# A decoder trunk on one core: the value and gate slabs of the mLSTM by seven products, in pieces between attention steps

## The reference

```python
h = rmsnorm(x, attn_norm_g)
(q, k_c, v_c, k_s, v_s, k_w, v_w, g_nsa, mq, mk, mv, mo, mi, mf, cu) = jnp.split(h @ w_in, points, axis=-1)
a_out = head_rmsnorm(nsa_attention(q, k_c, ..., g_nsa, ...), 16, nsa_out_g)      # width 1024
hm = mlstm_chunkwise(mq, mk, mv, mi + i_bias, mf + f_bias)                       # width 512
hm = head_rmsnorm(jax.nn.sigmoid(mo) * hm, 4, mlstm_out_g)
c = silu(layernorm(conv(ca * sigmoid(cg))))                                      # width 512
x = x + jnp.concatenate([a_out, hm, c], axis=-1) @ w_out
x = x + hier_moe(rmsnorm(x, ffn_norm_g), ...)                                    # 32 experts, 2 per token
return rmsnorm(x, final_norm_g)
```

## Time and profile before

| | us |
|---|---|
| median of 3 runs | 1427.34 |
| lowest, highest | 1425.18, 1428.28 |
| the profiled execution | 1428.03 |
| its span, first to last instruction | 1426.2 |

### The profile page before, as it was taken

One profiled execution on the slowest core, in us unless ns is written; L12 is line 12 of the kernel. 1 busy time (PEld: TensorE's weight loads), 2 busy tenths in 40 slices (PEclk: granted clock), 3 DMA queues, 4 the chain that ended last, 5 costly groups with the idle time before them and its releaser, 6 DMA issues.

```text
span 1426.2 us, 17903 instructions
## 1 busy us (share of the span) xinstructions
PE 1205.7 (85%) x7431; PEld 708.9 (50%) x7431; DVE 483.6 (34%) x1001; ACT 255.3 (18%) x629; POOL 13.5 (1%) x82
## 2 busy tenths in 40 slices
PE   8999999999999998669689958768587695876977
PEld 7999999766568753123244314224142241422422
DVE  5398997663875431121110220111101111011123
ACT  2101111444600122011111101002020010201112
POOL 2000000000010000000000000000000000000000
PEclk9999999999999999889999989989899898998989
DMA  9958677431644899999999999999999999999995
GB/s 318 274 158 194 167 161 236 119 82 38 165 112 166 346 413 426 429 427 427 428 428 428 426 428 427 427 427 429 428 426 427 429 427 425 431 426 426 429 427 237
DMA packets 133362, 479.34 MB, mean 336 GB/s; under 512 B 47804, under 2 KB 105632, under 8 KB 107552
## 3 DMA queue, kind: packets, MB, share of 16 engines
q1 hardware_dynamic: 126816, 477.58, 85.9%
q10 hardware_dynamic: 6464, 0.58, 0.4%
HBM read 476.05 MB, written 2.10 MB: 335 GB/s over the span
## 4 chain that ended last, share of the span: by engine, by line
PE 52%; DMA 43%; ACTq 2%; DVE 1%; ACT 1%; issue 1%; DVEq 0%
DMA ring<-in_expert_w_up_dram 36%; PE PS L1127 13%; PE PS L1447 10%; DMA spare<-in_expert_w_up_dram 6%; PE PS L1269 5%; PE PS L1169 3%; PE PS L1434 3%; PE PS L1246 2%; PE PS L1638 2%; ACTq L1862 2%; PE PS L1425 1%; PE PS L1221 1%; PE PS L1119 1%; PE PS L1648 1%; PE PS L1188 1%; PE PS L1509 1%
## 5 line engine op out<-in xcount | busy, mean ns | idle before, releaser
L1447 PE MATMUL PS<-ring,XG 128*32 128x512 f32 x1296 | 222.2, 734 | 147.9 <-DMA ring<-in_expert_w_up_dram 107.3
L1447 PEld LDWEIGHTS PS<-ring,XG 128*32 128x32 f32 x1296 | 57.6, 131 | 274.9 <-issue 271.8
L3068 DVE TENSOR_TENSOR hTe<-PS,sg 128x128 f32<-128x128 f32 (+1 forms) x31 | 9.9, 320 | 349.3 <-ACT sg L2193 349.1
L2885 DVE TENSOR_TENSOR x<-PS,x 128x1024 f32<-128x1024 f32 x41 | 50.2, 1225 | 209.8 <-PE PS L1526 208.4
L2181 ACT ACTIVATE Hs<-PS 128x512 f32<-128x512 f32 x30 | 17.9, 597 | 463.1 <-PE PS L1447 349.8
L1434 PE MATMUL PS<-ring,XG 128*64 128x512 f32 x192 | 84.6, 594 | 18.0 <-DMA ring<-in_expert_w_up_dram 14.5
L1526 PE MATMUL PS<-Y,SW 128*128 128x512 f32 (+2 forms) x176 | 90.6, 627 | 1.5 <-ACT ro L2289 1.5
L1447 PE MATMUL PS<-spare,XG 128*32 128x512 f32 x208 | 66.0, 793 | 27.8 <-DMA ring<-in_expert_w_up_dram 27.8
L1436 PE MATMUL PS<-ring,XG 128*64 128x512 f32 x192 | 85.0, 595 | 0.0
L1425 PEld LDWEIGHTS PS<-sel,xn 128*128 128x128 f32 x640 | 75.3, 191 | 13.0 <-issue 12.7
L1425 PE MATMUL PS<-sel,xn 128*128 128x128 f32 x640 | 77.6, 280 | 1.4 <-DVE x L2885 1.4
(11 more groups left out here) (494 smaller groups left out, 1577.2 us busy)
## 6 DMA issues: line engine op xcount, KB each, us to landing
ring<-in_expert_w_up_dram SPq DMA_DIRECT2D x53, 2048.0 KB, 23.8
ring<-in_expert_w_gate_dram SPq DMA_DIRECT2D x53, 2048.0 KB, 26.9
ring<-in_expert_w_down_dram SPq DMA_DIRECT2D x51, 2048.0 KB, 27.1
ring<-in_w_in_dram SPq DMA_DIRECT2D x17, 2048.0 KB, 9.5
spare<-in_expert_w_gate_dram SPq DMA_DIRECT2D x9, 2048.0 KB, 26.2
spare<-in_expert_w_up_dram SPq DMA_DIRECT2D x8, 2048.0 KB, 23.9
spare<-in_expert_w_down_dram SPq DMA_DIRECT2D x8, 2048.0 KB, 27.3
ring<-in_w_in_dram SPq DMA_DIRECT2D x16, 512.0 KB, 7.3
```

Of the source, the lines that this page charges most:

```text
L1447: mm = pe.matmul(PS[r:r + 32, 0, :], gathered_rows(q, 4 * c + j)[:, column:column + 32], weight_rows(slots[u], 4 * (c % 2) + j), start=(c ...
L2885: dve.tensor_tensor(y, new, old, ALU.add).then_inc(sc_added, 1)
```

## The change

The four late slabs join `FAST_SLABS`: they are made by the seven products too. A filler step is now a matmul of 128 columns, and there are 4 x 7 x 8 = 224 of them (before: 128 of 256 columns). The numbers of fillers given to each place are new. The four weight differences of slab 0 (`mv0`) are made by VectorE ahead of `biases(0)`, those of slabs 1 to 3 by GpSimd. The results are combined by VectorE in two parts, `late_first` (four operations) and `late_last` (four), placed between the pieces of the attention; ScalarE's eight copies go. `mlstm_values`, the output projection and the gate's sigmoid now wait for these combinations. Since the token sums stay needed in `x1`, the scores of odd steps lie in ring slot 1, and the differences in ring slot 2; so the pairs of slots of the output weights and of the expert chunks are renumbered. The second read of `x` is issued earlier, right behind the second pair of output weights. The third pair waits until the attention has turned its last block (before, it waited for units only, and the fourth had this wait); the fourth waits for `out_done`, as before. In the diff, "..." stands for lines left out: ScalarE's `late_saves` and its calls, and the branches of `save_unit` for `mv` and `mo`, are removed in them.

```diff
@@ -188,7 +188,8 @@
-FAST_SLABS = ("ca0", "ca1", "mq0", "mq1", "mk0", "mk1", "vc0", "ks0", "kw0", "vs0", "q0", "q1", "q2", "q3", "vw0")
+FAST_SLABS = ("ca0", "ca1", "mq0", "mq1", "mk0", "mk1", "vc0", "ks0", "kw0", "vs0", "q0", "q1", "q2", "q3", "vw0",
+              "mv0", "mv1", "mo0", "mo1")
 SUMS_BEFORE, PRODUCTS_BEFORE, TOKEN_SUMS = 4 * len(FAST), 2 * len(FAST), 4
...
 LATE = units_before("mv")
+LATE_SLABS = [u for u in FAST if u >= LATE]
+FAST_LATE = len(FAST) - len(LATE_SLABS)
+LATE_PRODUCTS = ["m2", "m1", "m6", "m7", "m5", "m3", "m4"]
+LATE_STEPS = 8 * len(LATE_PRODUCTS) * len(LATE_SLABS)
+SCALED = 2 + FAST_LATE
+LATE_SAVED = SCALED + 2 * len(LATE_SLABS)
...
-OUT_SLOTS = [(1, 2), (3, 4), (0, 5), (1, 2)]
+OUT_SLOTS = [(3, 4), (5, 0), (1, 2), (3, 4)]
...
-CHUNK_SLOT = [3, 4, 0, 5, 1, 2]
+CHUNK_SLOT = [5, 0, 1, 2, 3, 4]
...
-TURN = [SPARE, 3, 4, 0, 5, 1, 2]
+TURN = [SPARE, 5, 0, 1, 2, 3, 4]
...
         sc = [tile.rearrange("p (g h b k) -> p g h b k", g=2, h=HPG, b=2)
-              for tile in (att[:, :], x1[:, :, :].rearrange("p t d -> p (t d)"))]
+              for tile in (att[:, :], ring[:, 1, :, :].rearrange("p k n -> p (k n)"))]
...
+        late_sums = ring[:, 2, :, :].rearrange("p k n -> p (k n)").rearrange("p (s a k n) -> p s a k n", s=2, a=2, k=8)
+        late_a, late_b = upto[:, :], cmask[:, :]
+
+        def late_part(name):
+
+            q = LATE_PRODUCTS.index(name)
+            return PS[:, q // 4, P * (q % 4):P * (q % 4) + P]
...
             last_use = {n % RING: units_through(n) for n in range(len(SLABS))}
             for m, pair in enumerate(OUT_SLOTS):
-                if m < 3:
+                if m < 2:
                     sp.wait_ge(unit_done, max(last_use[s] for s in pair))
-                else:
-                    sp.wait_ge(p_turned, 2 * PAIRS_BY[-1])
+                elif m == 2:
                     for t in range(TT):
                         sp.dma_start(x1[:, t, :], x[0, t * P:(t + 1) * P, :]).then_inc(x_again, 16)
+                    sp.wait_ge(p_turned, 2 * PAIRS_BY[-1])
+                else:
                     sp.wait_ge(out_done, TT)
...
+            def late_sums_of(i):
+
+                j, u = FAST_LATE + i, LATE_SLABS[i]
+                n = UNITS[u][0]
+                pool.wait_ge(w_loaded[n % RING], slab_at[n])
+                pool.wait_ge(w_summed, 4 * j)
+                if i > 1:
+                    pool.wait_ge(unit_done, LATE_SLABS[i - 2] + 2)
+                pool.tensor_tensor(late_sums[:, i % 2, 0], quarter(u, 1, 1), quarter(u, 0, 1), ALU.subtract)\
+                    .then_inc(w_summed, 1)
+                pool.wait_ge(w_summed, 4 * j + 1)
+                pool.tensor_tensor(quarter(u, 0, 1), quarter(u, 0, 1), quarter(u, 0, 0), ALU.subtract)\
+                    .then_inc(w_summed, 1)
+                pool.wait_ge(w_summed, 4 * j + 2)
+                pool.tensor_tensor(late_sums[:, i % 2, 1], quarter(u, 1, 1), quarter(u, 0, 1), ALU.subtract)\
+                    .then_inc(w_summed, 1)
+                pool.wait_ge(prod_done, 2 * j + 1)
+                pool.wait_ge(w_summed, 4 * j + 3)
+                pool.tensor_tensor(quarter(u, 1, 0), quarter(u, 1, 0), late_sums[:, i % 2, 1], ALU.subtract)\
+                    .then_inc(w_summed, 1)
+
+            for i in range(1, len(LATE_SLABS)):
+                late_sums_of(i)
+
             pool.wait_ge(out_done, TT)
             step(pool.memset(lg_t, 0.0))
...
             def mlstm_values():
-                pe.wait_ge(unit_saved, units_with("mv"))
+                pe.wait_ge(first_scaled, SCALED + 4)
                 pe.wait_ge(biased, TILES_BY[-1])
...
             def late_step():
 
-                u, k = LATE + late[0] // DK, late[0] % DK
-                n, part, kind, s, i = UNITS[u]
+                i, r = divmod(late[0], 8 * len(LATE_PRODUCTS))
+                name, k = LATE_PRODUCTS[r // 8], r % 8
+                j, u = FAST_LATE + i, LATE_SLABS[i]
+                n = UNITS[u][0]
                 if k == 0:
-                    pe.wait_ge(w_loaded[n % RING], slab_at[n])
-                    pe.wait_ge(unit_saved, LATE - 2 if u == LATE else u - 1)
-                mm = pe.matmul(PS[:, unit_bank(u), 0:256], hT[:, k, i * P:(i + 1) * P], ring[:, n % RING, k, :],
-                               start=(k == 0), stop=(k == DK - 1))
-                if k == DK - 1:
+                    if name == "m2":
+                        pe.wait_ge(w_loaded[n % RING], slab_at[n])
+                    if name == "m2":
+                        pe.wait_ge(first_scaled if i else unit_saved, SCALED + 2 * i - 1 if i else LATE - 2)
+                    if name == "m5":
+                        pe.wait_ge(first_scaled if i else unit_saved, SCALED + 2 * i if i else LATE)
+                    if name in ("m6", "m4"):
+                        pe.wait_ge(w_summed, 4 * j + {"m6": 3, "m4": 4}[name])
+                tokens, weights = {"m1": (tok_11, quarter(u, 0, 0)), "m2": (tok_12, quarter(u, 1, 0)),
+                                   "m3": (tok_s4, quarter(u, 1, 1)), "m4": (tok_22, quarter(u, 1, 0)),
+                                   "m5": (tok_s1, quarter(u, 0, 1)), "m6": (tok_s2, late_sums[:, i % 2, 1]),
+                                   "m7": (tok_s3, late_sums[:, i % 2, 0])}[name]
+                mm = pe.matmul(late_part(name), tokens[:, k], weights[:, k], start=(k == 0), stop=(k == 7))
+                if k == 7 and name in ("m2", "m7"):
+                    mm.then_inc(prod_done, 1)
+                if k == 7 and name in ("m3", "m4"):
                     mm.then_inc(unit_done, 1)
                 late[0] += 1
...
-            fill(8)
+            fill(16)
             pe.wait_ge(unit_saved, LATE)
             pe.wait_ge(cmp_saved, 1)
-            scores(0, 2)
-            scores(1, 3)
-            fill(16)
+            scores(0, 6)
+            scores(1, 6)
+            fill(28)
             pe.wait_ge(sT_ready, ML_H)
-            attend(0, 4)
+            attend(0, 5)
             scores(2, 3)
-            attend(1, 4)
+            attend(1, 5)
             mean_square(0)
-            scores(3, 3)
+            scores(3, 5)
             fill(LATE_STEPS)
             mlstm_values()
             pe.wait_ge(conv_out, CT)
-            pe.wait_ge(unit_saved, len(UNITS))
+            pe.wait_ge(first_scaled, LATE_SAVED)
             out_part(0, conv_f, True, False)
...
-            exponents(0, 0)
-            late_saves(1)
-            exponents(1, 1)
-            late_saves(2)
-            attend_saves(0, 1)
-            exponents(2, 0)
-            late_saves(1)
-            attend_saves(1, 1)
+            exponents(0)
+            exponents(1)
+            attend_saves(0)
+            exponents(2)
+            attend_saves(1)
             head_root(0)
-            exponents(3, 0)
-            late_saves(1)
-            act.wait_ge(unit_saved, len(UNITS))
+            exponents(3)
+            act.wait_ge(first_scaled, LATE_SAVED)
             act.activation(mo[:, :, :], mo[:, :, :], ACT.Sigmoid, bias=ZERO_C).then_inc(mo_gated, 1)
             head_root(1)
-            attend_saves(2, 0)
-            attend_saves(3, 0)
+            attend_saves(2)
...
-            def biases(s):
+            def biases(s, slab=None):
...
                     dve.wait_ge(biased, 2 * pairs[0])
                     dve.tensor_reduce(rs[:, u, 0, :, i, 1:3], sc[u][:, :, i, :, 0:w], AX, ALU.max, negate=True)\
                         .then_inc(max_ready, 1)
+                    if i == 2 and slab is not None:
+                        late_first(slab)
...
-            biases(0)
-            biases(1)
+            def first_late_sums():
+
+                j, u = FAST_LATE, LATE_SLABS[0]
+                n = UNITS[u][0]
+                dve.wait_ge(w_loaded[n % RING], slab_at[n])
+                dve.wait_ge(unit_done, LATE)
+                dve.tensor_tensor(late_sums[:, 0, 0], quarter(u, 1, 1), quarter(u, 0, 1), ALU.subtract).then_inc(w_summed, 1)
+                dve.wait_ge(w_summed, 4 * j + 1)
+                dve.tensor_tensor(quarter(u, 0, 1), quarter(u, 0, 1), quarter(u, 0, 0), ALU.subtract).then_inc(w_summed, 1)
+                dve.wait_ge(w_summed, 4 * j + 2)
+                dve.tensor_tensor(late_sums[:, 0, 1], quarter(u, 1, 1), quarter(u, 0, 1), ALU.subtract).then_inc(w_summed, 1)
+                dve.wait_ge(prod_done, 2 * j + 1)
+                dve.wait_ge(w_summed, 4 * j + 3)
+                dve.tensor_tensor(quarter(u, 1, 0), quarter(u, 1, 0), late_sums[:, 0, 1], ALU.subtract).then_inc(w_summed, 1)
+
+            def late_first(i):
+
+                _, part, _, s, _ = UNITS[LATE_SLABS[i]]
+                dst, c = mv if part == "mv" else mo, 256 * s
+                dve.wait_ge(prod_done, 2 * (FAST_LATE + i) + 2)
+                step(dve.tensor_copy(late_a, late_part("m1")))
+                issued(dve.tensor_tensor(dst[:, 0, c:c + P], late_part("m2"), late_a, ALU.add))
```

(63 more changed lines are left out.)

## The result

| | before | after |
|---|---|---|
| median, us | 1426.55 (6 runs) | 1438.32 (6 runs) |
| lowest, highest | 1424.21, 1428.28 | 1436.93, 1440.05 |
| ratio of the times | | 1.008 (95%: 1.0069 to 1.0091) |
| the profiled execution | 1428.03 | 1440.05 |
| its span | 1426.2 | 1437.9 |

The change makes the kernel slower by 11.8 us. The forecast was slower by 4.1, with a range that ended at 1437.

What follows compares the result with a forecast made beforehand. TensorE at full clock was taken to bound the stretch. Passes and waits gave -1.6 us, GpSimd's holds +5.7, together +4.1: the median of 1427.34 becomes 1431.4, with a range of 1423 to 1437.

Steps and rivals of the forecast that it cites:

- Parts 1 and 2: TensorE's shorter filler passes (5.0 us back) and the attention stretch replayed against VectorE: sum -1.6 us.
- Part 3: SyncE's loads and the renumbered slots: output weights and `x` land before they are wanted, so nothing.
- part 4: GpSimd's twelve differences, 2.3 us each, hold up VectorE's scalings and two-tensor SBUF operations: 5.7 us taken, from 3.4 to 12.8.
- (a): Slab 1's last difference holds VectorE's L2630, ahead of late_last(0) and biases(1): 1.3 us taken, 3.8 with a second entry.
- (b): Slab 2's last difference and slab 3's three hold VectorE in gated(0), which attend(0) waits for: 4.3 us, two entries.
- (c): Slab 3's last difference, at scores(2)'s end, holds L2630 and reaches ScalarE's copies: 0.1 us.
- Rival B: VectorE isn't held up by GpSimd: 1425.7 us, with errors 1423.5 to 1427.5; chance 0.27.
- C: Faster outright, VectorE's new pieces find room everywhere: -6.6 us, half of it at least, 1421 to 1424; chance 0.10.
- D: GpSimd's operations take 3.3 us, every hold a microsecond longer: +7, up to +13, 1434 to 1440; chance 0.08.
- each time GpSimd can: In gated(0), GpSimd gets in at every chance: a hold of 8.9 us, where 4.3 was taken.
- worst case of both places: Upper end of the summed GpSimd holds on VectorE in the attention stretch: 12.8 us, where 5.7 was taken.

Runs made afterwards that it cites:

- the separated version: Changed kernel with one more wait ahead of GpSimd's last difference of each slab, behind VectorE's operations: 1424.97 us, ratio 0.9983 to before; second set 1425.33, 0.9992.
- only (b) separated: Changed kernel with one added wait: slab 2's last GpSimd difference waits until gated(1) is done: 1427.66 us, ratio 1.0005 to before.
- one operation at gated(0): Changed kernel with slab 3's three first GpSimd differences waiting until gated(1) is done, slab 2's last left in place: 1431.72 us, ratio 1.0035 to before.
- TensorE kept busy: Changed kernel with nine more matmuls, results unread, on TensorE ahead of attend(0): 1435.35 us, ratio 1.0061 to before.
- kernel with the fills: Changed kernel with GpSimd filling the twelve destinations with 0.0 instead of computing the differences: 1428.38 us, ratio 1.0007 to before.

## Why the prediction was right and wrong

Parts 1 and 2 held. The passes of 128 columns cost 1.53 for twelve and 1.31 for ten, with 1.54 and 1.32 worked out. The replay gave -1.6 for the stretch, and the separated version has -1.64. Its own steps can be read off against it, since it differs from the change only in the holds (its stage is 0.46 later in its profile, which is taken off here):

```profile
313.91 1.06 PE PS L1256 x8
...
369.99 1.14 PE PS L1290 x2
```

attend(0) begins at 313.45, as predicted to the hundredth (by luck to that degree), scores(2) at 329.4 (329.5), mean_square(1) at 369.5 (369.7). Part 3 held: in the kernel after TensorE waits for no transfer in the stretch nor in the products behind it, the part behind the stretch takes what it took before, and SyncE's waits for the products of the output projection are 62.3 us against the 62.6 of the earlier trace rows.

The mechanism of part 4 held too: GpSimd's operation takes 2.35 against the 2.3 taken between 1.0 and 3.3, VectorE is held in operations on one or two tensors within SBUF and in no other (not in the reductions, the reciprocal or those with an input from PSUM), and the places are (a), (b) and (c). Rival B (not held up) fell with the holds, C (faster outright) with the separated version's 1.65 instead of 3.3 to 6.6, and D (a larger operation) with the 2.35: the time measured lies in D's 1434 to 1440, but not by D's cause. Three steps failed:

- **The number of entries in (b).** Taken: one hold for L2644 and one in the scalings, 4.3, "since VectorE's scalings are issued back to back ... and should leave no gap for a third". Measured: 8.22, of which 6.41 in the scalings, with three entries of GpSimd. It got in each time that it had an operation ready; the case "each time GpSimd can", 8.9, stood in the text and was put aside by an argument about issue that no row supported. This step is 3.9 of the 7.7 by which the change costs more than forecast (11.8 against 4.1).
- **TensorE's clock.** No term at all. A wait of some 9 us on TensorE was implied by the worst case of (b), and the rows of before, with the clock at 1.00, have no wait over 0.5 in that stretch, so they couldn't speak for it. It costs 2.5. The run that keeps TensorE busy shows it: attend(0) in 16.0.
- **(a) and (c).** 1.3 became 1.55: the last difference starts 0.67 ahead of the held operation (288.75 against 289.42) and lasts 2.36, where 1.0 and 2.3 had been taken. The held operation was the one on eight elements, ahead of the one that I named. (c) was 0.1 and is 0.2 on the path, though the hold itself is 1.03: the rest is covered by the wait for ScalarE's copy.

The terms of part 4 thus read 1.55 + 8.22 + 0.23 + 2.53 = 12.5 where 5.7 stood, and -1.65 + 12.5 is the 10.9 of the stretch. The rest of the 11.8 between the medians, 0.9, is not explained by the stretch; it is within what the parts ahead of it and behind it vary by.

The range failed by the clock. With the case "each time GpSimd can" in (b) and one entry in (a), as it came, the prediction's own terms give -1.6 + 1.3 + 8.9 + 0.1 = +8.7, or 1436.0, inside the range; the 2.5 us of the clock, for which it had no term, carry it over 1437. The text had also worked out a worst case of both places, -1.6 + 12.8 = +11.2, 1438.5, and the range was cut inside it; but the second entry in (a), 2.5 of that sum, didn't come, so a range to 1438.5 would have been right by luck.

Open: what decides whether the clock falls after a short wait. Behind waits of 2.3 us it stayed at 1.00 in two profiles (after, and only (b) separated) and fell in two (one operation at gated(0), and TensorE kept busy); behind 2.7 it stayed, behind 3.3 and 9.1 it fell. Nor is it the same moment: with the waits of 9.1 and 3.3 it fell during the wait, with those of 2.3 only 0.5 and 1.2 us behind the wait's end. Whether this goes differently from one execution to the next of one kernel wasn't tried; so the times of these kernels may carry 1.5 to 2.7 us of it in some executions. The kernel with the fills hints at it, no more: its median is 3.05 above the separated version, where its profile has 5.20 more in the stretch and 2.57 without the clock.

## What to carry to other kernels

Work that GpSimd does in its idle time is free only if no VectorE operation of the held kinds (one-tensor operations within SBUF, such as the scalings, and beside differences those on two tensors there; a copy held GpSimd in the earlier trace rows, and whether GpSimd holds a copy no run shows) is both beside it and on the path. If several operations of GpSimd are ready one behind the other, count a full hold for each of them, however densely VectorE issues. Where VectorE must pass through such work in a known place, a wait that starts GpSimd's operation behind it costs nothing on the path where the operation's result isn't yet wanted: here one line gave back all of the loss of the stretch, and its part at (b) alone 10.8 of the 12.5. And a new wait on TensorE has a second price behind it, half the clock for some microseconds (3.4 to 10.2), seen here with waits from 2.3 to 9.1 us, though not with each of them.

## What the runs showed of the hardware that was not expected

- The two engines took turns: among scalings issued back to back, 0.27 apart, GpSimd entered three times in a row, 0.08 to 0.13 us after its own last end (313.13 + 2.50, then 315.71), and each of the three operations held one scaling, 2.14 apiece of the 6.41. With fills of 0.95 to 0.98 it did the same.
- A one-tensor operation on 8 elements a partition (0.17 us) is held for the whole rest of GpSimd's 2.36, as a large one is.
- VectorE's two-tensor operation ran in 0.18 beside a GpSimd fill, and in 1.99 beside a GpSimd difference.
- GpSimd's operation is longer by little, 2.43 and 2.50 instead of 2.35, where it started 0.06 to 0.07 us behind the start of a VectorE operation of these kinds (L2664 at 291.18, the first scaling at 313.07), which may be a hold the other way.
- TensorE's clock of 0.50 lasted 3.4 us where it fell after a wait of 2.3 (0.61 over the 4.40 from 292.30), and reached 5.2 us into the work behind the wait of 9.1 (0.83 over 328 to 332).
